# Two transformer blocks in one kernel: the weights of three modulation vectors are scaled and summed by GpSimd ahead of one product over the partitions

## The reference, cut to what matters

```python
mx = split(silu(c) @ w_mod + b_mod, 6)                 # shift, scale, gate, shift, scale, gate
hx = modulate(rmsnorm(x, g_norm1), mx[0], mx[1])
p  = hx @ w_in                                         # attention q, k, v and the recurrence's inputs
...                                                    # attention beside a gated recurrence in both directions
x = x + mx[2] * (concat([att_x, hg_x]) @ w_out)
x = x + mx[5] * swiglu(modulate(rmsnorm(x, g_norm2), mx[3], mx[4]), w_gu, w_down)
```

## Time and profile before

| | us |
|---|---|
| median of 3 runs (lowest, highest) | 821.33 (821.27, 821.45) |
| the profiled execution | 822.76 |
| its span, first to last instruction | 821.0 |
| PE busy | 795.5 (97%) |
| DVE busy | 429.1 (52%) |
| ACT busy | 418.8 (51%) |
| POOL busy | 377.1 (46%) |

### The profile page before, as it was taken

How to read it: one execution, slowest core, us unless ns; L and a number is a source line. 1 busy time by engine, 2 the same in 40 slices (tenths; PEclk the granted TensorE clock), 3 DMA queues, 4 the chain that set the end, 5 groups by cost and what they waited for, 6 DMA issues and landing times.

```text
span 821.0 us, 14292 instructions
## 1 busy us (share of the span) xinstructions
PE 795.5 (97%) x5493; PEld 693.6 (84%) x5493; DVE 429.1 (52%) x684; ACT 418.8 (51%) x641; POOL 377.1 (46%) x181
## 2 busy tenths in 40 slices
PE   5999999999899999999999999999999999999996
PEld 3778877887777999999998889999887988899985
DVE  4675569984566533332336747645456333423435
ACT  5335426455846444544444855654756544444443
POOL 3126000000164654566545986564464555666452
PEclk9999999999999999999999999999999999999999
DMA  9984567223943656555654796434455456566541
GB/s 321 310 274 138 162 240 245 59 97 109 358 148 106 205 182 202 179 179 184 195 167 134 224 208 180 130 107 132 148 171 164 157 183 196 180 193 189 188 146 51
DMA packets 94396, 146.61 MB, mean 179 GB/s; under 512 B 15741, under 2 KB 64110, under 8 KB 94352
## 3 DMA queue, kind: packets, MB, share of 16 engines
q1 hardware_dynamic: 92896, 143.23, 54.7%
q0 software_dynamic: 1424, 2.77, 1.2%
q10 hardware_dynamic: 32, 0.01, 0.0%
HBM read 144.93 MB, written 1.06 MB: 178 GB/s over the span
## 4 chain that ended last, share of the span: by engine, by line
PE 84%; DVE 6%; issue 3%; DMA 2%; POOL 2%; ACT 2%; SPq 0%; DVEq 0%; ACTq 0%; POOLq 0%
PE bank L1878 82%; POOL w_lo L629 2%; DMA raw<-in_w_mod 2%; PE bank L2148 1%; ACT w_hi L694 1%; DMA gate_mlp_b<-gate_rows 1%; PE bank L2456 1%; DVE x L1830 1%; DVE w_lo L1197 1%; DVE stat L1514 1%; DVE x L1643 0%; DVE o_lo L1735 0%; DVE bank L1642 0%; DVE probs L1474 0%; DVE hg_queries L1384 0%
## 5 line engine op out<-in xcount | busy, mean ns | idle before, releaser
L629 POOL TENSOR_TENSOR w_lo<-raw,w_hi 128x1024 fp32r<-128x1024 f32 (+2 forms) x150 | 362.0, 2429 | 318.4 <-ACT w_hi L694 318.2
L694 ACT ACTIVATE w_hi<-raw 128x1024 fp32r<-128x1024 f32 (+1 forms) x218 | 226.2, 1045 | 214.6 <-PE bank L1878 190.8
L1197 DVE TENSOR_TENSOR w_lo<-raw,w_hi 128x1024 fp32r<-128x1024 f32 x71 | 87.2, 1239 | 139.5 <-ACT w_hi L694 139.3
L1878 PE MATMUL bank<-z_hi,w_hi 128*128 128x256 f32 x384 | 108.8, 283 | 0.1
L1878 PE MATMUL bank<-z_hi,w_lo 128*128 128x256 f32 x384 | 107.4, 280 | 0.0
L1878 PE MATMUL bank<-z_lo,w_hi 128*128 128x256 f32 x384 | 107.1, 279 | 0.0
L1878 PE MATMUL bank<-n_hi,w_hi 128*128 128x256 f32 x352 | 98.6, 280 | 1.1 <-POOL w_lo L629 1.0
L1878 PE MATMUL bank<-n_hi,w_lo 128*128 128x256 f32 x352 | 98.4, 280 | 0.0
L1878 PE MATMUL bank<-n_lo,w_hi 128*128 128x256 f32 x352 | 98.1, 279 | 0.0
L1878 PE MATMUL bank<-w_hi,mlp_h_hi 128*128 128x512 f32 x216 | 85.6, 396 | 0.0
L1878 PE MATMUL bank<-w_lo,mlp_h_hi 128*128 128x512 f32 x216 | 85.4, 395 | 0.0
(11 more groups left out here) (419 smaller groups left out, 1554.7 us busy)
## 6 DMA issues: line engine op xcount, KB each, us to landing
raw<-in_w_in SPq DMA_DIRECT2D x54, 512.0 KB, 4.5
raw<-in_w_down SPq DMA_DIRECT2D x54, 512.0 KB, 3.6
raw<-in_w_gu SPq DMA_DIRECT2D x44, 512.0 KB, 3.5
raw<-in_w_up SPq DMA_DIRECT2D x32, 512.0 KB, 3.7
raw<-in_w_mod SPq DMA_DIRECT2D x24, 512.0 KB, 4.0
raw<-in_w_mod SPq DMA_DIRECT2D x32, 256.0 KB, 5.9
raw<-in_w_out SPq DMA_DIRECT2D x12, 512.0 KB, 3.8
raw<-in_w_in SPq DMA_DIRECT2D x8, 336.0 KB, 3.1
```

The costliest lines, as they stand in the source:

```text
L629: nc.gpsimd.tensor_tensor(wl[:, w % SPL, 0:size], raw[:, slot_raw, 0:size], wh[:, w % SPL, 0:size].bitcast(F32), ALU.subtract).then_inc(s_ ...
L694: nc.scalar.activation(wh[:, w % SPL, 0:size], raw[:, slot_raw, 0:size], ACT.Copy).then_inc(s_hi, 1)
L1197: V.tensor_tensor(wl[:, w % SPL, :], raw[:, slot_raw, :], wh[:, w % SPL, :].bitcast(F32), ALU.subtract).then_inc(s_lod, 1)
L1878: return nc.tensor.matmul(out_, l, r_, start=start, stop=stop, skip_group_check=True)
```

## The change

`mod_blocks` and the 256-column `mod_quarters` for the three vectors are gone from PE. In their place POOL does, for each chunk (`weighted`), a TENSOR_SCALAR that multiplies the chunk by silu(c) of its partition, in place in `raw`, and a TENSOR_TENSOR that adds it to a sum of 128x1024; the first chunk of each sum is multiplied straight into it. The sums are `ga1` for the gate, `ga2` for the shift, `kd` for the scale (free after `diag`). PE adds over the partitions at the end, with a stationary operand of ones: `gate_sums_out` (four products of 512 columns into bank 1, ahead of the transposes of q and k) and `scale_sums_out` (four of 256 into bank 5, in `hg_tail(9)`). ACT's copy "rows b" moves behind those of keysT and qT, the first scores wait for it, and the six bias DMAs into `ga1` and `ga2` move behind the gate sums. "acc" chunks stand in SP's order by `GATE_AT`.

```diff
+        GATE_AT = (1, 1, 2, 2, 1, 1, 1, 1, 2, 2, 2, 0, 0, 0)
+        gate_parts = [w_chunk(w_mod, i // 2, 1, 2048 + D * (i % 2), D) for i in range(2 * KT)]
...
-                if at_ < KT:
-                    add_acc(0, at_)
+                for i in range(GATE_AT[at_]):
+                    add("acc", gate_parts.pop(0))
...
+            def weighted(i):
+                k, j = (i // 2, i % 2) if i < 2 * KT else (i - 2 * KT, 2)
+                n = number["acc"][i]
+                sums = (ga1[:], ga2[:], flat(kd, 0, 4))[j]
+                arrived(pool, n)
...
+                if k == 0:
+                    ins = nc.gpsimd.tensor_scalar(sums, raw[:, n % RAW, :], csil[:, k, 0:1], None, ALU.mult)
+                else:
+                    nc.gpsimd.tensor_scalar(raw[:, n % RAW, :], raw[:, n % RAW, :], csil[:, k, 0:1], None, ALU.mult).then_inc(PL.sem, PL.tick(f"weighted {i}"))
+                    pool.wait_ge(s_acc, i - 1 if j < 2 else i)
+                    pool.wait_ge(PL.sem, PL[f"weighted {i}"])
+                    ins = nc.gpsimd.tensor_tensor(sums, sums, raw[:, n % RAW, :], ALU.add)
+                ins.then_inc(s_acc, 1)
...
+                while made < 2 * KT and number["acc"][made] < n:
+                    weighted(made)
+                    made += 1
+                if w == W_END["g"]:
+                    while made < 2 * KT + 5:
+                        weighted(made)
+                        made += 1
+                    pool.wait_ge(PE.sem, PE["gate sums"])
...
+                    while made < 3 * KT:
+                        weighted(made)
+                        made += 1
...
-            act.wait_ge(s_acc, 2 * KT)
-            nc.scalar.activation(rowb[:], ps[0][:], ACT.Copy).then_inc(AC.sem, AC.tick("rows b"))
...
+            act.wait_ge(PE.sem, PE["gate sums"])
+            nc.scalar.activation(rowb[:], ps[1][:], ACT.Copy).then_inc(AC.sem, AC.tick("rows b"))
...
+            def gate_sums_out():
+
+                pe.wait_ge(s_acc, 2 * KT)
+                for strip in range(4):
+                    ins = mm(ps[1][32 * strip:32 * strip + 32, :], ones[:, 0:32], (ga1 if strip < 2 else ga2)[:, 512 * (strip % 2):512 * (strip % 2) + 512], True)
+                ins.then_inc(PE.sem, PE.tick("gate sums"))
...
-            project("g", to_g, True, T, after=[between_first, between(1)], k_to=4)
+            project("g", to_g, True, T, k_to=4)
+            pe.wait_ge(AC.sem, AC["sig fb 3"])
...
-                for k in {0: (0,), 1: (1,), 3: (2,), 6: (3, 4), 8: (5, 6), 9: (7,)}.get(n, ()):
-                    c = number["acc"][2 * KT + k]
-                    arrived(pe, c)
-                    mod_quarters(k, 5, raw[:, c % RAW, :]).then_inc(s_acc, 1)
+                if n == 9:
+                    scale_sums_out()
```

More of the change, by code:

```diff
@@ L637, in gate_back @@
                 pool.dma_start(gate[:], a["gate_rows"][g:g + 1, :].broadcast_to([P, D])).then_inc(s_gb, 16)
-            for w, n in enumerate(number["w"]):
[L640 to L643, removed]
+            def weighted(i):
[3 more added lines that the diff above has]
+                arrived(pool, n)
+                if i == 0:
+                    pool.wait_ge(DV.sem, DV["csil"])
+                elif i == 2 * KT:
+                    pool.wait_ge(PE.sem, PE["diag 1"])
+                if k == 0:
[6 more added lines that the diff above has]
+                ins.then_inc(s_acc, 1)
+            made = 0
+            for w, n in enumerate(number["w"]):
+                while made < 2 * KT and number["acc"][made] < n:
[6 more added lines that the diff above has]
+                    pool.wait_ge(PE.sem, PE["gate sums"])
+                    for gate, c0, n_ in ((ga1, 2 * D, 512), (ga2, 5 * D, 256)):
+                        for j in range(D // n_):
+                            pool.dma_start(gate[32 * j:32 * j + 1, 0:n_], a["b_mod"][0:1, c0 + n_ * j:c0 + n_ * j + n_]).then_inc(s_gr, 16)
+                    while made < 3 * KT:
+                        weighted(made)
+                        made += 1
                 if w == W_END["kv"]:
@@ L653, in _ @@
                     pool.wait_ge(PE.sem, PE["hg out"])
+                    pool.wait_ge(PE.sem, PE["scale sums"])
                     pool.dma_start(gfin[:], a["g_final"].rearrange("(o n) -> o n", o=1).broadcast_to([P, D])).then_inc(s_gf, 16)
@@ L846, in hg_tail @@
                 elif n == 10:
-                    act.wait_ge(s_acc, 3 * KT)
+                    act.wait_ge(PE.sem, PE["scale sums"])
                     nc.scalar.activation(rowc[:], ps[5][:], ACT.Copy).then_inc(AC.sem, AC.tick("rows c"))
@@ L1947, in mod_rows, with scale_sums_out @@
                             ins.then_inc(s_mod, 1)
-            def mod_blocks(k, bank):
-                for j in range(2):
-                    arrived(pe, number["acc"][2 * k + j])
+            def gate_sums_out():
+                pe.wait_ge(s_acc, 2 * KT)
                 for strip in range(4):
[L1954 to L1958, removed]
+                    ins = mm(ps[1][32 * strip:32 * strip + 32, :], ones[:, 0:32], (ga1 if strip < 2 else ga2)[:, 512 * (strip % 2):512 * (strip % 2) + 512], True)
+                ins.then_inc(PE.sem, PE.tick("gate sums"))
+            def scale_sums_out():
+                pe.wait_ge(s_acc, 3 * KT)
+                for strip in range(4):
+                    ins = mm(ps[5][32 * strip:32 * strip + 32, 0:T], ones[:, 0:32], kd[:, strip, :], True)
+                ins.then_inc(PE.sem, PE.tick("scale sums"))
             def mod_quarters(k, bank, weights):
@@ L2083, in cross, with nothing @@
                 ins.then_inc(PE.sem, PE.tick("cross"))
[L2085 to L2091, removed]
+            def nothing():
+                pass
             to_g = [(ps[4 + j // 2][:, T * (j % 2):T * (j % 2) + T], j % 2 == 0) for j in range(4)]
             pe.wait_ge(DV.sem, DV["hq"])
-            def between_first():
-                pe.wait_ge(AC.sem, AC["sig fb 3"])
-                mod_blocks(0, 0)
-            project("g", to_g, True, T, after=[between_first, between(1)], k_to=4)
+            project("g", to_g, True, T, k_to=4)
+            pe.wait_ge(AC.sem, AC["sig fb 3"])
             project("kv", [(ps[2 + t // 2][:, T * (t % 2):T * (t % 2) + T], t % 2 == 0) for t in range(4)], False,
-                    after=[between(2, diag), between(3, lambda: level(0))])
+                    after=[diag, lambda: level(0)])
             pe.wait_ge(AC.sem, AC["kv 1"])
             project("q", [(ps[2 + t][:], True) for t in range(2)], False,
-                    after=[between(4), between(5, lambda: level(1)), between(6), between(7, lambda: level(2))])
+                    after=[nothing, lambda: level(1), nothing, lambda: level(2)])
             pe.wait_ge(AC.sem, AC["q 1"])
-            pe.wait_ge(AC.sem, AC["rows b"])
             project("i", [(ps[j][:], True) for j in range(4)], False,
@@ L2114, in _ @@
             pe.wait_ge(AC.sem, AC["val 3"])
+            gate_sums_out()
             for name, bank in (("keysT", 2), ("qT 0", 3), ("qT 1", 0)):
@@ L2131, in scores @@
                     pe.wait_ge(DV.sem, DV["qT 1"])
+                    pe.wait_ge(AC.sem, AC["rows b"])
                 else:
```

## The result

The changed kernel takes 861.49 us (859.91 to 863.60, four runs) against 821.30 us: 1.0488 times as long, interval 1.0475 to 1.0501. The forecast was 855 us with a range of 826 to 884. The profiled execution took 863.6 us, its span 861.8.

What follows compares the result with a forecast made beforehand. PE and DVE were taken as nearly even, DVE setting the pace after 131 us. The profiled 822.8 us + 34.0 (stretch) + 0.1 (attention) = 856.9, as a median 855 us; range 826 to 884.

Steps and rivals of the forecast that it cites:

- Part 3: Stretch 92 to 172 us: POOL's passes, one-operand ones included, block DVE for their whole length; 114.0 us for 80, +34.0.
- single pass: POOL's one-operand scaling of a 128x1024 chunk: 1.30 us, lower end 0.6, upper end 2.36.
- Part 2: Work coming to POOL: 24 chunks, 3.66 us a pair; 59.9 us of POOL from 92 us to the stretch's end.
- DVE's bank reads: Stretch from 92 us: two thirds of 14.1 us of DVE work can run beside POOL, 9.4 us off the bill.
- dearer passes: Rival, chance 0.13: one-operand passes cost as much as two, +18 us, 873; decided by a pass over 1.8 us.
- only two-operand passes exclude: Rival, chance 0.14: POOL's 17 one-operand passes do not block DVE, 22 us leave the bill, 833 us.
- half the operands, half the column's time: Sizing of POOL's one-operand pass: 1.02 ns a column instead of 2.05, plus 0.26 us start, 1.30 us.
- Part 1: Work leaving PE: about 9 us in the projections, counted at nothing; 4.1 us on the path in the attention.
- the plan works: Rival, chance 0.10: no exclusion where it counts; DVE's waits close, -8.2 us, attention gives 1.9; median 811 us.
- Part 4: Small terms: slots, g_qk and bias DMAs covered, row copy 0.6 us, three last pairs; attention as a whole 0.1 us.
- term of 2 us for the three pairs: Attention: the last three pairs, 11.0 us of POOL beside a DVE mostly on banks, priced at 2 us.
- covered by a few us: The two g_qk DMAs behind POOL's unit 5, about 100 us, land some 4 us later, before DVE reads them.

Runs made afterwards that it cites:

- empty passes: Changed kernel with both POOL passes cut to 8 of 1024 columns, the first pass of each sum whole: 812.39 us, ratio 0.9872.

## Why the prediction came out

**Part 3, the exclusion, was right for the add, and it decides.** The forecast had DVE stand still for 59.9 - 9.4 - 6.6 = 43.9 us; it stood still for 40.8. The stretch grew by 33.2 us, forecast 34.0. With POOL's passes nearly empty 49 us go, and DVE's lengths come back. For the scaling pass Part 3 was wrong: DVE does not stand aside for its length. The Trainium skill (SBUF — State Buffer, Who interferes with whom) has the two engines shut each other out for a whole instruction; this trace agrees for the add (2.84 us for 0.69) and not for the scaling pass, beside which two operations of DVE get through.

**The single pass was mis-sized twice, in Part 2 and in Part 3, and the errors nearly cancel.** I had it at 1.30 us (ends 0.6 and 2.36) and blocking for its whole length, 1.1 us each behind the hand-over. It takes 2.85 us undisturbed, beyond the upper end, and costs DVE some 0.6 us. With the right length and the rule of Part 3 the forecast would have been some 26 us higher (17 x 1.55), near 881 us, so that the stretch came out is in part luck. Measured against empty passes, DVE loses 9.5 us to 16 of the 17 scaling passes and 31.8 to the adds; the forecast had 18.7 for 17 and 34.6, some 11 us too much, and the 9.4 us that it took off for DVE's bank reads bring it near again: 43.9 against 41.3. By its own rule the rival "dearer passes" had to win, as the pass is over 1.8 us; it gave 873 us and did not, since the length is not what DVE pays. The rival "only two-operand passes exclude" gave 833 us (836 with the hand-overs of the 17 passes given back, which its sum left in): it is out too, by the 12.2 us of the scaling pass, and because the adds alone already take 845 us. Why a pass that also reads and writes SBUF lets DVE through is not shown by any run. The lesson of the step is in its ground: "half the operands, half the column's time" had no row, and the estimate by the Trainium skill (GPSIMD Engine Reference, Performance versus the Vector engine), 0.9 to 1.1 us, is further off still.

**Part 1 was right.** PE's 9 us in the projections count nothing as things stand: PE waits for DVE's w_lo for 25.5 us. What the change could have given, with the attention's share, is the 8.9 us of the empty passes, against 10.1 us by the rival "the plan works" (8.2 and 1.9).

**Part 4: the attention failed.** Its 0.1 us net covers all from DVE's last key to MLP 1, and that grew by 6.5 us. Up to the first scores the forecast had the gate sums and the copy, 1.0 + 0.6 = 1.6 us, and 3.0 came. Behind them it had -4.1 + 0.6 + 2 = -1.5 us, and +3.5 came. The term of 2 us for the three pairs is what failed: taking them out gives 6.6 us, and without them PE's way from the scores to MLP 1 is 3.0 us shorter than before, forecast 3.5. The term counted DVE's work there as bank reads, while the probabilities are on the path and stop for an add. g_qk "covered by a few us" is wrong by a wait of 1.2 us, and whether that costs anything stays open. "Covered" was also said of SP's slots, for units of 3.66 us; that holds at 2.9 us and fails at 5.9, by 25 us, so for the true pair it was luck that DVE came last (ACT waits for `raw` for 3.4 us in the changed kernel).

**Not priced: the clock.** The granted clock is 1.00 in the stretch before and 0.85 after: behind its waits PE runs at the lower of its two levels (1.2 GHz), where products of 512 columns follow each other at 0.43 us (from 180.68 us on) instead of 0.23 (at 170.19). Most of it lies under DVE's pace. On the path it is at the end: behind its last wait for w_lo PE's products of 256 columns follow each other at 0.21 us up to 200.48 us and at 0.12 behind it, so 5.5 us are spent on what takes 3.1 at the upper level. I put some 2 us of the 3.0 between DVE's last key and the first scores to it, what the gate sums' 1.0 us leave. That is argued from these steps; no run isolated it. The rows right behind a wait of 7.1 us show the lower level, in the timeline of PE after; a product of 256 columns has a mean of 0.28 us in MLP 1, whose clock is full:

```profile
194.98 0.58 PE L1911 MATMUL bank<-h_hi,w_hi 128*128 128x256 f32 x1 [7.14 <-DVE w_lo L1230]
195.36 0.42 PE L1911 MATMUL bank<-h_lo,w_hi 128*128 128x256 f32 x1
```

The sum was 855 and the time 861.5. By the landmarks the difference is -0.8 us in the stretch, +1.4 up to the first scores, +5.0 from there to MLP 1 and +1.1 behind it, 6.7 us in the profiled execution and 6.5 between the medians.

## What to carry to other kernels

Before work is given to an idle engine, ask which engine its operations make stand still, and whether that one has room: here POOL's 100 free us cost 2.0 us of DVE for each add and 0.6 for each scaling pass between 92 us and its last key, where DVE set the pace, and 1.7 us in all for four units beside an idle DVE. What an operation costs its neighbour is a number of its own, not its length; take both from rows or measure both. And an engine in the middle of a chain of slots can have a longest unit that the ring allows, here between 2.9 and 5.9 us, whatever its share of busy time.

## What was not expected of the hardware

- POOL's TENSOR_SCALAR of 128x1024 f32 takes 2.85 us, longer than its TENSOR_TENSOR of the same shape with two tensor operands (2.36 us), and a constant in place of the factor per partition does not make it short (2.79 us).
- It makes DVE lose some 0.6 us of those 2.85 on the mean; the add makes it lose 2.0 of 2.36.
- POOL's writing of 128x1024 takes 0.98 us and leaves DVE's w_lo (1.21 us) and keys (0.68 us) alone, while a TENSOR_SCALAR of 128x2048 of DVE takes 1.98 us instead of 1.23 beside it.
